# A two-layer Fourier and convolution backbone with experts: slab steps behind routers and table, row tiles weighted ahead of the norm, last output tile by column halves

## The reference

```python
for i in range(DEPTH):                                   # DEPTH = 2
    sh1, sc1, g1, sh2, sc2, g2 = jnp.split((silu_c @ w_ada[i] + b_ada[i])[:, None, :], 6, axis=-1)
    hx = _rmsnorm(x, norm_mix[i]) * (1 + sc1) + sh1
    yx = _fourier_mix(hx, fourier_w_out[j])              # layer 0
    yx = _short_conv_mix(hx, conv_w_in[j], conv_w[j], conv_w_out[j])     # layer 1
    x = x + g1 * yx
    hx = _rmsnorm(x, norm_ffn[i]) * (1 + sc2) + sh2
    y = _moe(hx.reshape(-1, d), router_w, router_bias, moe_w_gate[i], moe_w_up[i], moe_w_down[i])
    x = x + g2 * y.reshape(b, l, d)

def _moe(h, router_w, router_bias, w_gate, w_up, w_down):
    scores = jax.nn.sigmoid((h @ router_w).astype(jnp.float32))
    # top 2 experts within the best of 4 groups; weights w = their scores over the sum of both
    for e in range(N_EXPERTS):
        he = jax.nn.silu(h @ w_gate[e]) * (h @ w_up[e])
        y = y + comb[:, e:e + 1] * (he @ w_down[e])
```

## Time and profile before

| | us |
|---|---|
| median of 3 runs | 1144.11 (1143.71 to 1147.41) |
| the profiled execution | 1146.1 |
| its span | 1144.2 |
| PE busy | 1080.6 (94%) |
| DVE busy | 800.0 (70%) |
| ACT busy | 487.5 (43%) |
| POOL busy | 178.2 (16%) |

### The profile page before, as it was taken

How to read it: one execution, slowest core, us unless ns; L and a number is a source line. 1 busy time by engine, 2 the same in 40 slices (tenths; PEclk the granted TensorE clock), 3 DMA queues, 4 the chain that set the end, 5 groups by cost and what they waited for, 6 DMA issues and landing times.

```text
span 1144.2 us, 14933 instructions
## 1 busy us (share of the span) xinstructions
PE 1080.6 (94%) x4747; PEld 793.4 (69%) x4747; DVE 800.0 (70%) x968; ACT 487.5 (43%) x677; POOL 178.2 (16%) x135
## 2 busy tenths in 40 slices
PE   4999999899999999789999999999999899999994
PEld 2554446577777776368888888878887577777772
DVE  5886997788888888266434434454574788888893
ACT  5211135277667765461111111142232366677661
POOL 2101111122222233200000000000000122233331
PEclk9989999999999999999999999999999999999997
DMA  9878649677989974713733223313133978999853
GB/s 367 321 271 313 256 188 414 227 261 204 309 266 298 346 224 111 231 54 111 276 117 123 80 85 128 128 40 144 74 132 149 365 253 264 325 355 280 259 114 47
DMA packets 82002, 243.48 MB, mean 213 GB/s; under 512 B 10016, under 2 KB 34808, under 8 KB 72700
## 3 DMA queue, kind: packets, MB, share of 16 engines
q1 hardware_dynamic: 62436, 188.88, 43.8%
q0 software_dynamic: 17920, 48.31, 16.6%
q10 hardware_dynamic: 1560, 5.26, 1.2%
HBM read 218.29 MB, written 40.89 MB: 227 GB/s over the span
## 4 chain that ended last, share of the span: by engine, by line
PE 75%; DVE 11%; DMA 6%; issue 3%; ACT 2%; ACTq 1%; DVEq 0%; POOL 0%; SPq 0%; POOLq 0%
PE PS L1980 21%; PE PS L1858 8%; PE PS L2093 7%; PE PS L2094 7%; PE PS L2097 7%; PE PS L1993 6%; PE PS L1999 5%; PE PS L1970 4%; DVE ACC L1159 3%; PE PS L1709 3%; PE PS L1671 2%; DMA WAE<-in_w_ada_dram 2%; PE PS L1873 1%; DMA x_dram<-YO,TOKI 1%; ACT SQ L747 1%
## 5 line engine op out<-in xcount | busy, mean ns | idle before, releaser
L1480 DVE TENSOR_TENSOR WL<-RAW,WH 128x1024 fp32r<-128x1024 f32 x192 | 225.6, 1218 | 0.6 <-ACT WH L936 0.4
L936 ACT ACTIVATE WH<-RAW 128x1024 fp32r x184 | 184.6, 1052 | 36.6 <-issue 26.0
L1980 PE MATMUL PS<-WH,XTH 128*128 128x512 f32 x368 | 147.2, 400 | 4.5 <-issue 4.5
L1980 PE MATMUL PS<-WH,XTL 128*128 128x512 f32 x368 | 144.1, 391 | 0.0
L2093 PE MATMUL PS<-HTH,WINH 128*128 128x512 f32 x368 | 143.3, 389 | 0.3 <-DVE WINL L1566 0.3
L1980 PE MATMUL PS<-WL,XTH 128*128 128x512 f32 x368 | 143.5, 390 | 0.0
L2094 PE MATMUL PS<-HTL,WINH 128*128 128x512 f32 x368 | 143.2, 389 | 0.0
L2097 PE MATMUL PS<-HTH,WINL 128*128 128x512 f32 x368 | 113.2, 389 | 0.0
L1993 PE MATMUL PS<-WDR,HETF 128*128 x184 | 88.6, 605 | 4.8 <-DVE YO L1494 4.3
L1494 DVE SCALAR_TENSOR_TENSOR YO<-PS,WOF,ROWS 128x1024 f32<-128x1024 f32 x46 | 59.1, 1284 | 41.6 <-PE PS L1999 30.6
L663 POOL DMA_INDIRECT XG<-h_dram,TOKI x50 | 58.4, 1168 | 174.2 <-PE PS L1970 117.4
(11 more groups left out here) (251 smaller groups left out, 1762.3 us busy)
## 6 DMA issues: line engine op xcount, KB each, us to landing
RAW<-in_moe_w_gate_dram SPq DMA_DIRECT2D x32, 1024.0 KB, 6.7
RAW<-in_moe_w_up_dram SPq DMA_DIRECT2D x32, 1024.0 KB, 10.3
WDR<-in_moe_w_down_dram SPq DMA_DIRECT2D x32, 1024.0 KB, 10.2
WA<-in_w_ada_dram SPq DMA_DIRECT2D x28, 1024.0 KB, 7.7
WAE<-in_w_ada_dram SPq DMA_DIRECT2D x12, 1024.0 KB, 9.3
WINR<-in_conv_w_in_dram SPq DMA_DIRECT2D x24, 512.0 KB, 3.8
SLAB<-in_w_ada_dram SPq DMA_DIRECT2D x8, 1024.0 KB, 12.1
X<-x_dram SPq DMA_DIRECT2D x16, 512.0 KB, 5.1
```

The lines of the kernel that those rows point to most:

```text
L936: nc.scalar.activation(piece_of(WH[par], i), raw_piece(at, i), ACT.Copy).then_inc(w_high, 1)
L1480: V.tensor_tensor(piece_of(WL[par], i), raw_piece(e, i), piece_of(WH[par], i).bitcast(f32), ALU.subtract).then_inc(w_low, 1)
L1980: ins = T.matmul(bank(2), x[:, ch, :], w[par][:, :, ch, :], start=ch == 0 and i == 0, stop=ch == NC - 1 and i == 2)
```

## The change

Three edits, on PE, ACT and DVE, with the numbers in the waits of SP and POOL adapted to them.

1. **Slab steps.** In layer 0 slabs 0 to 5 come after the last router (they stood between the routers, two of them after the last), in place of `keep_running(3)`. Slabs 6 and 7 come after the 16 table matmuls, in place of a `keep_running(1)`; they stood before them. DVE waits for all slabs before `weights_low(0)`.
2. **Weighted ahead.** `hidden(m)` becomes `weighted(m)`, XS = X * GS2, and `shifted(m)`, H = XS * RS + SH2. In layer 0 `weighted(6)` and `weighted(7)` stand ahead of `rstd`, and in layer 1 `weighted(7)` ahead of `last_rstd`.
3. **Last tile by halves.** In layer 1 the product of tile 7 is made for columns 0 to 511 first, then for the others, with a semaphore step after each; residual and squares of tile 7 follow by halves.

```diff
@@ scalar
+            def last_squares():
+                m = NT - 1
+                for half in range(2):
+                    cols = slice(half * BANK, (half + 1) * BANK)
+                    act.wait_ge(x_ready, 2 * NT + half)
+                    norms["squares"] += 1
+                    nc.scalar.activation(SQ[:, cols], X[:, m, cols], ACT.Square,
+                                         accum_out=(SS, RT)[half][:, m:m + 1]).then_inc(sq_done, 1)
+                    act.wait_ge(sq_done, norms["squares"])
...
                 for m in range(3, 6):
                     transposed(m)
-                square_of(7)
+                last_squares()
                 root(NORMS[3])
@@ vector
+            def last_added():
+                m, b = NT - 1, 2
...
+                for half in range(2):
+                    cols = slice(half * BANK, (half + 1) * BANK)
+                    dve.wait_ge(y_mm, 2 * NT + half)
+                    link(V.tensor_tensor(XS[m % 2][:, cols], bank(b + half), G1[:, cols], ALU.mult))
+                    V.tensor_tensor(X[:, m, cols], X[:, m, cols], XS[m % 2][:, cols], ALU.add).then_inc(x_ready, 1)
...
+            def last_rstd():
...
+                dve.wait_ge(sq_done, norms["squares"] - 1)
+                link(V.tensor_scalar(var, SS[:, m:m + 1], 1.0 / D, EPS, ALU.mult, ALU.add))
+                dve.wait_ge(sq_done, norms["squares"])
+                V.scalar_tensor_tensor(out=var, in0=rt, scalar=1.0 / D, in1=var, op0=ALU.mult, op1=ALU.add).then_inc(var_ready, 1)
...
+            def weighted(m):
...
+                link(V.tensor_tensor(XS[m % 2][:], X[:, m, :], GS2, ALU.mult))
+
+            def shifted(m):
...
+                V.scalar_tensor_tensor(out=h_tile(layer, m)[:], in0=XS[m % 2][:], scalar=RS[:, m:m + 1], in1=SH2,
+                                       op0=ALU.mult, op1=ALU.add).then_inc(h_ready, 1)
...
                 pair(3)
+                weighted(6)
+                weighted(7)
                 rstd(NORMS0[2])
-                hidden(6)
-                hidden(7)
+                shifted(6)
+                shifted(7)
...
-                branch_added(7)
-                rstd(NORMS[3])
-                hidden(7)
+                last_added()
+                weighted(7)
+                last_rstd()
+                shifted(7)
...
             dve.wait_ge(routed, layer + 1)
+            if layer == 0:
+                dve.wait_ge(slab_used, NC)
             weights_low(0, 0, place_of(layer, 0))
```

More of the change, by code:

```diff
@@ L646, in store_x @@
         def store_x(layer, m):
-            pool.wait_ge(x_ready, layer * NT + m + 1)
+            pool.wait_ge(x_ready, layer * NT + m + 1 + (layer and m == NT - 1))
             if layer == 0 and m % 2:
@@ L911, in _ @@
             sigmoids(1)
-            act.wait_ge(y_mm, NT * (layer + 1))
+            act.wait_ge(y_mm, NT * (layer + 1) + layer)
             wait_loaded(act, layer, 0, 32, raw3_in)
@@ L1280, in branch_added @@
                     tile_low(m + 2)
-            def hidden(m):
+            def last_added():
+                m, b = NT - 1, 2
+                dve.wait_ge(h_ready, hiddens[0])
+                dve.wait_ge(x_ready, 2 * NT - 2)
+                dve.wait_ge(x_back[m], 32)
+                for half in range(2):
[3 more added lines that the diff above has]
+                    V.tensor_tensor(X[:, m, cols], X[:, m, cols], XS[m % 2][:, cols], ALU.add).then_inc(x_ready, 1)
+                residuals[0] = 2 * NT + 1
+            def last_rstd():
+                m = NT - 1
+                var, rs, rt = VAR[:, m:m + 1], RS[:, m:m + 1], RT[:, m:m + 1]
+                norms["squares"] += 2
+                norms["roots"] += 1
+                dve.wait_ge(sq_done, norms["squares"] - 1)
+                link(V.tensor_scalar(var, SS[:, m:m + 1], 1.0 / D, EPS, ALU.mult, ALU.add))
+                dve.wait_ge(sq_done, norms["squares"])
+                V.scalar_tensor_tensor(out=var, in0=rt, scalar=1.0 / D, in1=var, op0=ALU.mult, op1=ALU.add).then_inc(var_ready, 1)
+                dve.wait_ge(sd_ready, norms["roots"])
+                link(V.reciprocal(rs, SD[:, m:m + 1]))
+                link(V.tensor_tensor(rt, rs, rs, ALU.mult))
+                link(V.tensor_tensor(rt, rt, var, ALU.mult))
+                link(V.tensor_scalar(rt, rt, -0.5, 1.5, ALU.mult, ALU.add))
+                V.tensor_tensor(rs, rs, rt, ALU.mult).then_inc(rs_ready, 1)
+                dve.wait_ge(rs_ready, norms["roots"])
+            def weighted(m):
+                dve.wait_ge(x_ready, residuals[0] if layer else 2 * pairs[0])
+                if hiddens[0]:
+                    dve.wait_ge(h_ready, hiddens[0])
+                link(V.tensor_tensor(XS[m % 2][:], X[:, m, :], GS2, ALU.mult))
+            def shifted(m):
                 if layer and m >= 4:
@@ L1286, in hidden @@
                     dve.wait_ge(h_tr, n0 + m - 3)
[L1287 to L1289 removed]
                 hiddens[0] += 1
[L1291 to L1293 removed]
+                V.scalar_tensor_tensor(out=h_tile(layer, m)[:], in0=XS[m % 2][:], scalar=RS[:, m:m + 1], in1=SH2,
+                                       op0=ALU.mult, op1=ALU.add).then_inc(h_ready, 1)
+            def hidden(m):
+                weighted(m)
+                shifted(m)
             if layer == 0:
@@ L1860, in conv_out, with conv_out_last @@
             ins.then_inc(y_mm, 1)
+        def conv_out_last():
+            m, b = NT - 1, 2
+            pe.wait_ge(x_ready, NT + m - 1)
+            pe.wait_ge(z_low, m + 1)
+            for h in range(2):
+                for ch in range(NC):
+                    for i, (z, w) in enumerate(((ZH, WOH), (ZH, WOL), (ZL, WOH))):
+                        ins = T.matmul(bank(b + h), z[m % 2][:, ch, :], w[:, ch, h * BANK:(h + 1) * BANK],
+                                       start=ch == 0 and i == 0, stop=ch == NC - 1 and i == 2)
+                ins.then_inc(y_mm, 1)
         for layer in range(2):
@@ L1901, in _ @@
                 hidden_transposed(m + 1)
-                if layer == 0 and m == 3:
-                    mixer_slab(0)
-                    mixer_slab(1)
                 router(m)
             if layer:
-                conv_out(NT - 1)
+                conv_out_last()
             hidden_transposed(5)
@@ L1915, in _ @@
                 hidden_transposed(6)
-                mixer_slab(2)
             router(6)
@@ L1922, in _ @@
                 keep_running(1)
-            if layer == 0:
-                mixer_slab(3)
             router(7)
@@ L1928, in _ @@
             if layer == 0:
-                mixer_slab(4)
-                mixer_slab(5)
-            keep_running(4 if layer else 3, spare)
+                for k in range(6):
+                    mixer_slab(k)
+            else:
+                keep_running(4, spare)
             pe.wait_ge(rounded, layer + 1)
@@ L1957, in _ @@
             ins.then_inc(table_mm, 1)
-            keep_running(1, 4)
+            if layer == 0:
+                mixer_slab(6)
+                mixer_slab(7)
+            else:
+                keep_running(1, 4)
             pe.wait_ge(weight_hot, 2 * (layer + 1))
```

11 lines of the change are left out of this document (1 added, 10 removed).

## The result

| | before | changed |
|---|---|---|
| median, us | 1146.61 (1143.71 to 1148.88, 13 runs) | 1152.34 (1147.33 to 1155.88, 13 runs) |
| ratio, 95% | | 1.0053 (1.0039 to 1.0066) |
| profiled execution, us | 1146.1 | 1150.68 |
| its span, us, and mean clock | 1144.2, 0.985 | 1148.9, 0.978 |

The change makes the kernel 5.7 us slower by the medians, 4.7 by the two spans. I had forecast 1.4 faster. Against the later median of before, 1146.61 instead of 1144.11, my forecast would read 1145.2 and the upper end of my range 1149.3 instead of 1146.8; 1152.34 lies above both. The ratio with its interval is estimated from the runs of both kernels and can differ a little from the quotient of the medians.

The account below looks back on a forecast made before the run. PE, busy 94% of the span, was taken as the bound, so only its waits counted. Layer 0 +0.7 us and layer 1 -2.1 made -1.4, from a median of 1144.1 to 1142.7 us; range 1140.4 to 1146.8.

Parts of the forecast that it names:

- The clock: 1.06 more, and 0.3 more: Layer 0: half clock after PE's emptied wait at the router of tile 3 costs 1.06 us, at the table 0.3.
- The third rival: Layer 0 routers and transposes at half clock throughout, up to 7 us instead of 1.06; total +4.6, 1148.7 us; chance 0.10.
- VAR at 179.75 (forecast 179.6, +1.28 of 1.45): Layer 0: two weighting instructions ahead of VAR delay it, the root and ACT's copies by 1.45 us.
- the wait on PE: Layer 0, ahead of the router of tile 3: PE idle 3.6 us with slabs 0 and 1 gone, half clock expected behind.
- slabs 0 to 5 ahead of the mask cost nothing: Layer 0: four more slabs, 3.9 us, replace keep_running(3) and a wait, together 4.0; no change.
- slab loads: Layer 0: SP starts loading slabs 6 and 7 about 11 us later, near 200, so the gather meets the bulk's tail.
- the gather of layer 0: Gather beside bulk loads takes 5.5 us instead of 4.33; with 1.0 in hand, +0.2 us.
- the table's 2.33: Layer 0: with slabs 6 and 7 behind it, the table starts when ROWHOT is there, 2.33 us sooner.
- first expert matmul 0.56 sooner: Layer 1, relative to PE's last output matmul: first expert matmul forecast 2.1 us sooner.
- The gather term: Layer 1: bulk loads end 1.6 us earlier, so the gather shortens by 1.1 us, from 6.30 to near 5.2.
- DVE, whose bound I had worked out as 905.9: Layer 1: DVE alone would allow the first expert matmul at 905.9, beside 906.0 by the gather.
- The Trainium skill's rule: Layer 0: each burst of matmuls after a wait starts at half rate; both falls 1.06 us, 0.8 more than taken.

Follow-up runs that it names:

- slabs only: Kernel before with only the slab steps moved as in the change; 1156.3 us against 1146.71, ratio 1.0067.
- fill router: Changed kernel with three keep_running matmuls in PE's wait ahead of the router of tile 3 in layer 0; 1148.69 us, ratio 1.0026.
- routers back: Changed kernel with slabs 0 to 3 back between the routers, 4 and 5 behind the last with keep_running(3); 1152.19 us, ratio 1.005.
- layer 1 only: Kernel before with only layer 1's edits, last tile by halves and tile 7 weighted ahead; 1146.3 us, ratio 0.9992.
- weighted only: Kernel before with only tiles 6 and 7 weighted ahead of the norm in layer 0; 1148.36 us, ratio 1.0012.
- fill all: Changed kernel with keep_running matmuls ahead of the routers of tiles 3, 6 and 7, and four instead of two ahead of the table; 1145.67 us, ratio 0.9989.
- table only: Kernel before with only slabs 6 and 7 moved behind the table, two keep_running ahead of it; 1146.9 us, ratio 1.0.

## Why the prediction was wrong

**The step that failed** is "The clock: 1.06 more, and 0.3 more". I took the price of a fall from two slabs that lost 1.06 us, and not from the work that stands behind the wait. VAR to the sigmoids is a chain of routers and transposes with nothing beside it, so what the clock takes there, the chain loses: +3.11 in the changed kernel's trace (12.00 to 15.11), +6 where the fall lasted (slabs only and fill router, 18.0 and 18.1). At the table I gave it 0.3; it cost 1.93 in the trace (6.06 against 4.13 at full clock), up to 6.8 in the slowest trace of routers back and in the second of the changed kernel. Layer 1 had no such term, and lost 1.5, by a fall that the kernel before can have as well. With these three sizes in place of 1.06 and 0.3, the sum is -1.4 - 1.36 + 3.11 + 1.93 + 1.5 = +3.8, against +4.7 between the spans; the rest, 0.9, is the stretches without an edit (0.28 late at X, 0.80 regained, 1.67 lost).

**The third rival**, "the clock stays low over the router stretch", was the right mechanism. Even it was priced short: it ended the damage at the sigmoids (up to 7 more), and in slabs only the half clock went on through routers 6 and 7, for 15.6 in all with the table. Its argument against itself, that PE is back at work between the waits, is what the trace of slabs only contradicts: with waits of 1.21 us, and routers and transposes between them, the clock was not back until past 206. In the changed kernel's two traces the fall ended by 188, in the middle of the stretch, so that the rival's +4.6 lies near the measured loss by other terms than its own. The chance of 0.10 was too low also because I weighed only that size; shorter falls in three places give nearly the same total.

**What was right**, by the trace: VAR at 179.75 (forecast 179.6, +1.28 of 1.45); the wait on PE with a clock of 0.5 behind it (3.27 of 3.6); slabs 0 to 5 ahead of the mask cost nothing (0.52 of wait left where 1.17 was), though not where the fall lasts (slabs only); slab loads at 201.8 (near 200); the gather of layer 0 5.4 us (5.5), and +0.1 for it (+0.2); the table's 2.33, which every trace with the table at full clock shows exactly (6.46 to 4.13) and neither trace of the changed kernel gets. In layer 1, relative to PE's last output matmul: H 1.6 sooner, the first expert load at 879.56, so 1.6 sooner (6.52 after it instead of 8.09); sigmoids 0.16 sooner (0.2); first expert matmul 0.56 sooner, and 2.10 sooner where no fall is (the trace of layer 1 only), the forecast. VAR came 0.3 sooner, as taken. The gather term was wrong in it: it took 4.26 us in the changed kernel and 4.33 in layer 1 only, where I had taken 5.2. The total came out because DVE, whose bound I had worked out as 905.9 beside 906.0, then set the start: XTL begins at 909.79, as soon as DVE is done with WOF, its instruction ahead of it, at 909.57 + 0.19. By its time alone layer 1 only, at 1146.3 against 1146.71, would not show the 2.1.

**The Trainium skill's rule**, TensorE: Matmul & The Clock Gate, HAM oscillation (a kernel whose bursts of matmuls have waits for transfers between them started every burst at half rate), would have given 0.8 more than I took. The changed kernel's trace agrees that both falls come; the router of weighted only, at 1.98 us behind a wait of 1.90, does not start at half rate. The size still was not in it, since I priced it by the same two slabs.

**The measurement's own bound.** I had counted on one trace standing for the kernel. Single executions of one kernel lie up to 12 to 15 us apart here (slabs only, routers back), in part by how long a fall lasts, and one trace shows one draw. Not all of it is the falls: the changed kernel's second trace has X to XTL 54.6 us, 4.6 more than its first, and took only 0.8 more in all, and over the 18 traces the stretch from layer 0's first expert matmul to layer 1's last output matmul, in which the edits only change the order of tile 7's matmuls, takes from 644.8 to 648.7 us. Over kernels the median goes roughly with the mean clock of the runs: 0.970 for slabs only, 0.975 for the changed kernel, 0.981 to 0.982 for the one before, 0.982 for fill all, 0.983 to 0.984 for the three at 1144 to 1145.

**Still open.** Why 10 of 12 runs of routers back lie over 1150 and only 1 of 12 of table only, when both have two fillers at the table. They differ in the weighting and in layer 1. The trace of 1149.58 shows the router fall, which the longer wait under the weighting allows, that of 1150.57 a long table fall without it. How often each happens was not counted, and why a fall is short or long stays open.

## What to carry to other kernels

Before work is moved out of a wait of PE, ask what stands behind the wait. If it is a chain of matmuls that others wait for, the moved work may have been holding the clock up, and what is at stake is the length of that chain and not the length of the work moved. Where work has to go, leave `keep_running` in its place, sized to end just ahead of the release; two fillers with a wait of 2.3 us behind them were too few, four, with 0.6 of wait or none left, kept the table at or near full clock in six traces. Move a long transfer's consumer and its fillers in one edit, take three or more traces of a kernel whose times spread, and price a clock fall from the rows of the chain at both levels.
